# Loading the first layer's eight parameter rows from ScalarE's queue instead of the sync engine's

## The chip, the cores and the metric

The kernel runs on one core of a Trainium2 chip. The core has five engines with an instruction stream each: TensorE (PE in the rows, with its weight loads as PEld), VectorE (DVE), ScalarE (ACT), GpSimd (POOL) and the sync engine (SP). Two of these streams, SP's and ScalarE's, issue the transfers between the chip's memory and the on-chip buffers in this kernel; 16 DMA engines carry them. The metric is the device time in microseconds, the median of several runs.

## The reference

Two transformer-like blocks are applied to one sequence of 256 tokens with 2048 channels, all in float32. The first block has two layers, the second has one. What matters here is how the first one begins:

```python
def first_block(x, w_in, conv_w, conv_b, conv_ln_g, conv_ln_b, pool_w, pool_scale, g_mix,
              w_out, g_pre_mix, g_post_mix, g_pre_ffn, g_post_ffn, w_gate, w_up, w_down):
    ...
    for l in range(DEPTH):
        h = rmsnorm(x, g_pre_mix[l])
        proj = h @ w_in[l]
        y_a = conformer_conv(proj[..., :a_end], conv_w[l], conv_b[l], conv_ln_g[l], conv_ln_b[l])
        y_b = dilated_attention(proj[..., a_end:b_end], cos, sin)
        y_c = pool_mixer(proj[..., b_end:], pool_w[l], pool_scale[l])
        y = jnp.concatenate([rms_normalize(y_a), rms_normalize(y_b), rms_normalize(y_c)], axis=-1)
        y = (y * g_mix[l].astype(jnp.float32)).astype(x.dtype)
        x = x + rmsnorm(y @ w_out[l], g_post_mix[l])
        h = rmsnorm(x, g_pre_ffn[l])
        f = (jax.nn.silu(h @ w_gate[l]) * (h @ w_up[l])) @ w_down[l]
        x = x + rmsnorm(f, g_post_ffn[l])
    return x
```

The eight parameters that the change is about are `g_pre_mix`, `g_pre_ffn` (2048 numbers each), `g_mix` (2048), `conv_b`, `conv_ln_g`, `conv_ln_b`, `pool_scale` (512 each) and `conv_w` (31 taps by 512 channels) of layer 0. Of these only `g_pre_mix` is wanted at once: it scales the channels of x before the first product with `w_in`.

## The kernel before

All weights stream through a ring of four slots `WS` of 512 KB (128 partitions x 1024 numbers). Each such unit is split into a high and a low part: ScalarE copies it to `WH` in the rounded format (line 859) and VectorE forms the rest, `WL` (line 1480). TensorE then makes three products for each tile of weights and activations (line 2057). The activations `XT` are x turned by TensorE (line 2157), scaled by the column `g_pre_mix` and split in the same way: ScalarE writes the high part (line 874), VectorE the low one (line 1496).

The order of the work on each engine is written out by hand; each engine runs its own stream in that order and waits on semaphores.

At the beginning the streams are these.

- SP issues, in this order: the first constants (`C`, with the identity that TensorE needs for turning), columns 0 to 511 of x (two transfers, one for each half of the tokens), weight unit 0, then, after a wait for VectorE's clearing of `ROWS` (`s_eps`), the eight parameter rows of layer 0, then columns 512 to 1023 of x, weight unit 1, columns 1024 to 2047 of x, and units 2, 3 and so on as slots come free.
- GpSimd only passes on the arrival of x: one semaphore step when the first 512 columns are there, and all the other steps when all the rest of x is (line 1742).
- ScalarE loads its table for the square root (line 959), splits unit 0, copies the turned parameter rows to `PR` (lines 906 and 907) and then makes the high parts of the first four tiles of `XT`; then it splits unit 1, makes four more tiles, and splits three more units.
- TensorE turns the first eight 128x128 pieces of x, turns the two halves of `ROWS` (line 2177), multiplies unit 0 (24 matmuls of 256 columns), turns eight more pieces of x, multiplies unit 1, turns eight, and so on.
- VectorE clears `ROWS` and writes the small constants, makes `WL` of unit 0, and then the low parts of `XT`.

A row of parameters is first a row of `ROWS` (128 numbers in one partition) and becomes a column only by TensorE's turning. TensorE waits for all eight transfers together before it turns `ROWS`:

```python
            def layer_params(l, bank):

                pe.wait_ge(s_rows, 16 * 8 * (l + 1))
                for r in range(2):
                    pe.transpose(PS[:, bank, r * P:(r + 1) * P], ROWS[:, r, :], ident).then_inc(s_prt, 1)
```

Of the kernel before, what the change touches and what calls it, by code (L numbers as in the profile page):

```python
# [14 lines left out]
P = 128  # L15
# [75 lines left out]
TAPS = 31  # L91
# [41 lines left out]
def build(nc, a, out, stop=None):  # L133
    with ExitStack() as ctx:  # L134
        def sb(name, shape, dt=F32):
            return ctx.enter_context(nc.sbuf_tensor(name, shape, dt))

        def sem(name):
            return ctx.enter_context(nc.semaphore(name))
# [17 lines left out]
        ROWS = sb("ROWS", [P, 2, P])  # L157
# [141 lines left out]
        s_const, s_const2, s_xload, s_eps = sem("s_const"), sem("s_const2"), [sem("s_xload0"), sem("s_xload1")], sem("s_eps")  # L299
        s_rows, s_prt, s_par = sem("s_rows"), sem("s_prt"), sem("s_par")  # L300
# [37 lines left out]
        def turn_planes(queue, planes):  # L338

            for w in range(2):  # L340
                for t in range(NT):
                    queue.dma_start_transpose(plane_chan[:, w, :, t * P:(t + 1) * P], planes[:, w, t, :]).then_inc(s_turned, 16)

        @block.sync
        def _(sp):
            def load(q, i, src, width, turn=None):

                sp.wait_ge(s_lo, 4 * q + i + 1)
                if turn:
                    sp.wait_ge(s_words, turn[0])  # L350
                dst = WS[:, i % RING, :]
                if width:
                    dst = dst.rearrange("p (k n) -> p k n", n=width)
                sp.dma_start(dst, src).then_inc(s_stage[i % RING], 16)
                if turn:
                    turn_planes(sp, turn[1])

            def chunk512(q, w, c, first=False, turn=None):

                for i in range(8):  # L360
                    load(q, i, w[2 * i * P:(2 * i + 2) * P, c].rearrange("(k p) n -> p k n", p=P), CHUNK,
                         turn if turn and i == turn[2] else None)
                    if first and i == 0:
                        sp.wait_ge(s_eps, 1)
                        layer_rows(0)
                        x_columns(1, 512, 1024)
                    if first and i == 1:
                        x_columns(1, 1024, 2048)

            def out_proj(q, w):  # L370
                for c in range(2):
                    for i, kt in enumerate(OUT_ORDER):
                        load(q, 16 * c + i, w[kt * P:(kt + 1) * P, c * 1024:(c + 1) * 1024], 0)

            def down_proj(q, w, turns, between=None):

                rows = w.rearrange("(r k p) n -> r k p n", k=4, p=P)

                def four(c, r, turn=None):
                    for i in range(4):  # L380
                        load(q + r + 11 * c, i, rows[r, i, :, c * 1024:(c + 1) * 1024], 0, turn if turn and i == turn[2] else None)

                for c in range(2):
                    if c and between:
                        between()
                    for r in range(0 if c else 3):
                        four(c, r, turns.get(r))
                    with sp.Fori(0 if c else 3, FKT // 4) as r:
                        four(c, r)
# [27 lines left out]
                sp.dma_start(a_log, a["gdn_a_log_2"].to_broadcast((P, 4))).then_inc(s_rows2, 16)  # L417
                sp.dma_start(dt_bias, a["gdn_dt_bias_2"].to_broadcast((P, 4))).then_inc(s_rows2, 16)

            def layer_rows(l):  # L420

                small = [("g_pre_mix", 16), ("g_pre_ffn", 16), ("g_mix", 16), ("conv_b", 4), ("conv_ln_g", 4),
                         ("conv_ln_b", 4), ("pool_scale", 4)]
                at = 0
                for name, n in small:
                    sp.dma_start(ROWS[at:at + n, 0, :], a[name][l].rearrange("(n p) -> n p", p=P)).then_inc(s_rows, 16)
                    at += n
                sp.dma_start(ROWS[0:4 * TAPS, 1, :], a["conv_w"][l].rearrange("j (n p) -> (j n) p", p=P)).then_inc(s_rows, 16)

            def x_columns(part, c0, c1):  # L430
                for t in range(NT):
                    sp.dma_start(x[:, t, c0:c1], a["x"][0, t * P:(t + 1) * P, c0:c1]).then_inc(s_xload[part], 16)
# [3 lines left out]
            for l in range(DEPTH):  # L436
                q = l * (U_LAYER // 4)
                w = a["w_in"][l]
                for n, c in enumerate(IN_ORDER):
                    if (l, n) == (0, 1):  # L440
                        sp.dma_start(C[:, 2 * P:C_END], a["constants"][:, 2 * P:C_END]).then_inc(s_const2, 16)
                    chunk512(q + 2 * n, w, slice(c * CHUNK, (c + 1) * CHUNK), l + n == 0)
                q1 = q + U_IN1 // 4
                out_proj(q1, a["w_out"][l])
                q2 = q1 + U_OUT // 4
                def glu_loads(j, turn=None):
                    chunk512(q2 + 4 * j, a["w_gate"][l], bass.ds(j * CHUNK, CHUNK))
                    chunk512(q2 + 4 * j + 2, a["w_up"][l], bass.ds(j * CHUNK, CHUNK), turn=turn)

                glu_loads(0)  # L450
                with sp.Fori(1, 11) as j:
                    glu_loads(j, (22 * l + 2 * j - 1, plane_tok, 2))
                q3 = q2 + U_UP // 4
                if l < DEPTH - 1:
                    sp.wait_ge(s_prt, 2 * (l + 1))
                    layer_rows(l + 1)
                down_proj(q3, a["w_down"][l], {2: (22 * l + 21, plane_tok, 2)}, second_rows if l == DEPTH - 1 else None)

            q = DEPTH * (U_LAYER // 4)
# [394 lines left out]
        def _(act):  # L854
# [79 lines left out]
            def post_squares_last(q, m, n_units, bank):  # L934

                act.wait_ge(s_sf, 6 * m + 2)
                for t in range(NT):
                    for n in range(2):
                        if (t, n) == (1, 1):
                            product_done(q, 2 * n_units - 1)  # L940
                        else:
                            act.wait_ge(s_bank, 3 * m + 2 * t + n + 1)
                        act.activation(junk[3 - t][:, n * CHUNK:(n + 1) * CHUNK], PS[:, bank(1, t) + n, :], ACT.Square,  # L943
                                       accum_out=ssf[:, 3 * t + 1 + n:3 * t + 2 + n]).then_inc(s_sf, 1)
                    post_root(m, t)

            def wide_phase(q, m, n_units, first=4, last=False, bank=out_bank, params=None):
# [7 lines left out]
                splits(q, n_units + (PARAMS_AT if params else 0) + 4, 2 * n_units + (0 if last else 2))  # L955
                post_squares_last(q, m, n_units, bank)

            act.wait_ge(s_eps, 2)
            act.activation(root_junk, epsc, ACT.Sqrt)
            split(0, 0)  # L960
# [2 lines left out]
            for l in range(DEPTH):  # L963
# [6 lines left out]
                for c in range(9):  # L970
# [12 lines left out]
                    if 2 <= c < 8:  # L983
                        n = c - 2
# [1316 lines left out]
```

## Time and profile before

| what | value |
|---|---|
| median of 3 runs | 3275.39 us (3275.04 to 3275.43) |
| span of the profiled execution | 3273.7 us |
| TensorE busy | 3251.2 us, 99% of the span |
| VectorE busy | 2042.7 us, 62% |
| ScalarE busy | 1631.5 us, 50% |
| DMA, mean | 191 GB/s |
| first matmul of the first product | 10.21 us after the span's start |

The profiled execution's own time is known as its span only, 3273.7 us from the first instruction's start to the last one's end; the medians are taken from runs without a profile, and the median lies 1.7 us above the span. Busy times are shares of the span, so an engine at 99% leaves 22.5 us in which it did nothing. The rows speak of the wait ahead of an instruction group as "idle before", with an arrow to what ended it.

### The profile page before, as it was taken

Reading aid. Unit: us, or ns where it says so; the run is one execution under the profiler, and the core shown is the slowest. Engines: PE = TensorE matmul, PEld = TensorE weight load, DVE = VectorE, ACT = ScalarE, POOL = GpSimd, SP = SyncE. Lnnn points to the kernel's source line nnn. Section 1 sums busy time; section 2 is a strip of 40 time slices with the busy share of each in tenths; the row PEclk is TensorE's granted clock in tenths of the full one; section 3 lists DMA queues with packets and bytes.
Section 4 is the critical chain, followed back from the end, with each engine's and each line's share of the span. In section 5 each row is a group of like instructions: output and inputs, shape, how many; then the busy total and the mean of one; then the engine's idle time right before and its main releaser. Section 6 shows DMA issues by size and latency. Waiting matters only on the chain. (4 is left out here: it accounts for less than half of the span.)

```text
span 3273.7 us, 43491 instructions
## 1 busy us (share of the span) xinstructions
PE 3251.2 (99%) x16149; PEld 2756.5 (84%) x16149; DVE 2042.7 (62%) x2449; ACT 1631.5 (50%) x2039; POOL 263.2 (8%) x180
## 2 busy tenths in 40 slices
PE   9999999999999999999999999999999999999999
PEld 8888888888888988888888888899898888888887
DVE  6876655555444787665555544477665677777544
ACT  5565544444443556554444444365554655555443
POOL 0000011111000000001111100000000122222000
PEclk9999999999999999999999999999999999999999
DMA  7545566767756554557676766645346677777654
GB/s 231 180 136 168 180 205 207 206 206 202 218 194 193 187 181 129 173 181 205 205 205 206 207 212 198 192 150 176 116 156 204 193 218 213 218 217 216 218 194 161
DMA packets 364799, 626.70 MB, mean 191 GB/s; under 512 B 117912, under 2 KB 120445, under 8 KB 364669
## 3 DMA queue, kind: packets, MB, share of 16 engines
q1 hardware_dynamic: 359693, 615.49, 61.6%
q10 hardware_dynamic: 4976, 9.44, 0.9%
q8 instruction: 87, 1.43, 0.2%
q14 instruction: 43, 0.35, 0.0%
HBM read 599.66 MB, written 2.10 MB: 184 GB/s over the span
## 5 line engine op out<-in xcount | busy, mean ns | idle before, releaser
L1480 DVE TENSOR_TENSOR WL<-WS,WH 128x1024 fp32r<-128x1024 f32 x1120 | 1426.4, 1278 | 1083.2 <-ACT WH L859 1082.3
L859 ACT ACTIVATE WH<-WS 128x1024 fp32r<-128x1024 f32 x1120 | 1184.2, 1060 | 1502.6 <-PE PS L2057 1473.5
L2057 PE MATMUL PS<-WH,XT 128*128 128x512 f32 x5952 | 1830.4, 391 | 0.5 <-ACT XT L874 0.5
L2057 PEld LDWEIGHTS PS<-WH,XT 128*128 128x128 f32 x5952 | 1116.9, 188 | 231.9 <-issue 1.1
L2057 PE MATMUL PS<-WL,XT 128*128 128x512 f32 x2976 | 1128.7, 389 | 0.0
L2057 PEld LDWEIGHTS PS<-WL,XT 128*128 128x128 f32 x2976 | 559.0, 188 | 114.0
L2057 PE MATMUL PS<-WH,HT 128*128 128x512 f32 x2112 | 567.8, 389 | 0.0
L2057 PEld LDWEIGHTS PS<-WH,HT 128*128 128x128 f32 x2112 | 396.3, 188 | 82.5 <-DVE WL L1480 0.2
L2057 PE MATMUL PS<-XT,WH 128*128 128x256 f32 x1792 | 336.5, 286 | 2.5 <-ACT XT L874 1.4
L2057 PE MATMUL PS<-WL,HT 128*128 128x512 f32 x1056 | 327.2, 389 | 0.0
L2057 PEld LDWEIGHTS PS<-XT,WH 128*128 128x128 f32 x1792 | 283.8, 192 | 4.6 <-ACT PR L907 1.4
L2057 PE MATMUL PS<-XT,WL 128*128 128x256 f32 x896 | 254.1, 284 | 0.0
L2057 PEld LDWEIGHTS PS<-WL,HT 128*128 128x128 f32 x1056 | 198.2, 188 | 41.0
L1748 POOL COPY T<-T 128x1024 uint16<-128x1024 uint16 x44 | 66.4, 1539 | 1532.1 <-DVE T L1154 1532.1
L2057 PEld LDWEIGHTS PS<-XT,WL 128*128 128x128 f32 x896 | 172.6, 193 | 0.1
L1757 POOL COPY SCR<-SCR 128x1024 uint16<-128x1024 uint16 x44 | 44.6, 1045 | 761.6 <-ACT SCR L808 761.6
L1596 DVE SCALAR_TENSOR_TENSOR SCR<-SCR,PR 128x256 f32<-128x256 f32 x240 | 101.1, 478 | 0.0
L2057 PE MATMUL PS<-SCR 128*128 128x256 f32 (+3 forms) x648 | 100.1, 300 | 0.5 <-DVE SCR L1335 0.5
L1752 POOL COPY T<-XL 128x1024 uint16<-128x1024 uint16 x44 | 76.3, 1781 | 240.2 <-DMA XL<-T 240.2
L1763 POOL COPY T<-XL 128x1024 uint16<-128x1024 uint16 x44 | 75.6, 1764 | 247.3 <-DMA XL<-SCR 247.3
L2057 PEld LDWEIGHTS PS<-SCR 128*128 128x128 f32 (+1 forms) x648 | 88.6, 191 | 7.7 <-DVE SCR L1335 0.9
L1428 DVE SCALAR_TENSOR_TENSOR T<-T,C 128x256 f32<-128x256 f32 x176 | 73.4, 478 | 9.2 <-ACT T L815 9.2
(277 smaller groups left out, 1176.7 us busy)
## 6 DMA issues: line engine op xcount, KB each, us to landing
WS<-in_w_in_dram SPq DMA_DIRECT2D x232, 512.0 KB, 3.6
WS<-in_w_gate_dram SPq DMA_DIRECT2D x176, 512.0 KB, 3.5
WS<-in_w_up_dram SPq DMA_DIRECT2D x176, 512.0 KB, 3.7
WS<-in_w_down_dram SPq DMA_DIRECT2D x176, 512.0 KB, 4.4
WS<-in_ffn_up_dram SPq DMA_DIRECT2D x176, 512.0 KB, 4.2
WS<-in_w_out_dram SPq DMA_DIRECT2D x96, 512.0 KB, 4.1
WS<-in_ffn_down_dram SPq DMA_DIRECT2D x88, 512.0 KB, 3.7
T<-in_g_post_mix_dram ACTq DMA_DIRECT2D x4, 512.0 KB, 5.8
```

What stands on the lines that cost most here:

```text
L859: act.activation(WH[:, i % RING, :], WS[:, i % RING, :], ACT.Copy).then_inc(s_hi, 1)
L1428: ins = dve.scalar_tensor_tensor(out=f3((T2, T3)[g])[:, n, :], in0=ffn_pad[:, n, k:k + S], scalar=conv_j[:, k, g, n:n + 1], in1=f3((T2, T3 ...
L1480: dve.tensor_tensor(WL[:, i % RING, :], WS[:, i % RING, :], WH[:, i % RING, :].bitcast(F32), ALU.subtract).then_inc(s_lo, 1)
L1596: dve.scalar_tensor_tensor(out=acc[:, n, :], in0=hpad[:, n, j:j + S], scalar=w, in1=acc[:, n, :], op0=ALU.mult, op1=ALU.add).then_inc(s_cv, 1)
L1748: ins = pool.tensor_copy(plane_tok[:, w, :, :], h_words[:, :, :, w])
L1752: ins = pool.tensor_copy(hT_words[:, :, :, w], plane_chan[:, w, :, :])
L1757: ins = pool.tensor_copy(ffn_planes[:, w, :, :], ffn_words[:, :, :, w])
L1763: ins = pool.tensor_copy(pad_words[:, :, :, w], plane_chan[:, w, :, :])
L2057: return pe.matmul(o, w, r, start=start, stop=stop, skip_group_check=True)
```

## The change

SP no longer issues the eight row transfers of layer 0, nor waits for `s_eps`. ScalarE does: its stream begins with a wait for the first step of `s_eps` (VectorE's clearing of `ROWS`), then the eight transfers, and only then the table load and all that was there before. The function is moved out so that both engines can call it; the rows of layer 1 are still loaded by SP. The semaphore that counts the arrivals is the same.

```diff
+        def layer_rows(queue, l):
+
+            small = [("g_pre_mix", 16), ("g_pre_ffn", 16), ("g_mix", 16), ("conv_b", 4), ("conv_ln_g", 4),
+                     ("conv_ln_b", 4), ("pool_scale", 4)]
+            at = 0
+            for name, n in small:
+                queue.dma_start(ROWS[at:at + n, 0, :], a[name][l].rearrange("(n p) -> n p", p=P)).then_inc(s_rows, 16)
+                at += n
+            queue.dma_start(ROWS[0:4 * TAPS, 1, :], a["conv_w"][l].rearrange("j (n p) -> (j n) p", p=P)).then_inc(s_rows, 16)
+
...
                     if first and i == 0:
-                        sp.wait_ge(s_eps, 1)
-                        layer_rows(0)
                         x_columns(1, 512, 1024)
                     if first and i == 1:
                         x_columns(1, 1024, 2048)
...
-            def layer_rows(l):
...
                     sp.wait_ge(s_prt, 2 * (l + 1))
-                    layer_rows(l + 1)
+                    layer_rows(sp, l + 1)
...
+            act.wait_ge(s_eps, 1)
+            layer_rows(act, 0)
             act.wait_ge(s_eps, 2)
             act.activation(root_junk, epsc, ACT.Sqrt)
             split(0, 0)
```

SP's stream from its first transfer, before. `WS` is the ring of weight slots, `x` the input, `C` the constants, `ROWS` the parameter rows:

```order
L434 DMA C<-in_constants_dram 128x256
L432 DMA x<-in_x_dram 128x512 x2
L354 DMA WS<-in_w_in_dram 128x2x512
L426 DMA ROWS<-in_g_pre_mix_dram 16x128
L426 DMA ROWS<-in_g_pre_ffn_dram 16x128
L426 DMA ROWS<-in_g_mix_dram 16x128
L426 DMA ROWS<-in_conv_b_dram 4x128
L426 DMA ROWS<-in_conv_ln_g_dram 4x128
L426 DMA ROWS<-in_conv_ln_b_dram 4x128
L426 DMA ROWS<-in_pool_scale_dram 4x128
L428 DMA ROWS<-in_conv_w_dram 124x128
L432 DMA x<-in_x_dram 128x512 x2
```

And SP's stream from the same place, now:

```order
L432 DMA C<-in_constants_dram 128x256
L430 DMA x<-in_x_dram 128x512 x2
L364 DMA WS<-in_w_in_dram 128x2x512
L430 DMA x<-in_x_dram 128x512 x2
L364 DMA WS<-in_w_in_dram 128x2x512
L430 DMA x<-in_x_dram 128x1024 x2
L364 DMA WS<-in_w_in_dram 128x2x512 x6
```

Weight unit 1 and the later columns of x stand directly behind unit 0 now.

ScalarE's stream at its beginning, now. Before, it began with the table load of line 959:

```order
L350 DMA ROWS<-in_g_pre_mix_dram 16x128
L350 DMA ROWS<-in_g_pre_ffn_dram 16x128
L350 DMA ROWS<-in_g_mix_dram 16x128
L350 DMA ROWS<-in_conv_b_dram 4x128
L350 DMA ROWS<-in_conv_ln_g_dram 4x128
L350 DMA ROWS<-in_conv_ln_b_dram 4x128
L350 DMA ROWS<-in_pool_scale_dram 4x128
L352 DMA ROWS<-in_conv_w_dram 124x128
L959 ACT_TABLE_LOAD
L959 ACTIVATE SM<-SM 128x1
L857 ACTIVATE WH<-WS 128x1024
```

The eight transfers stand ahead of the table load and so ahead of the split of unit 0 (now line 857). The streams of TensorE and VectorE have the same instructions in the same order as before.

## Rows read from the trace of the kernel before

**Rows 1.** The page: TensorE's busy time in the whole span
```profile
PE 3251.2 (99%) x16149; PEld 2756.5 (84%) x16149; DVE 2042.7 (62%) x2449; ACT 1631.5 (50%) x2039; POOL 263.2 (8%) x180
```

**Rows 2.** TensorE's waits, whole span: us in total, times, longest us
```profile
PE PS L2157 <- POOLq L1742: 6.4, 2, 5.9
PE PS L2157 <- DVE x L1562: 3.9, 5, 0.8
PE PS L2057 <- ACT XT L874: 1.9, 6, 1.1
PE PS L2177 <- DMA ROWS<-in_conv_w_dram: 0.6, 1, 0.6
```

**Rows 3.** Timeline of TensorE: start us, us, group, idle before
```profile
5.89 1.94 PE L2157 MATMUL PS<-C,x 128*128 128x128 f32 x8 [5.89 <-POOLq L1742]
8.44 0.69 PE L2177 MATMUL PS<-C,ROWS 128*128 128x128 f32 x2 [0.61 <-DMA ROWS<-in_conv_w_dram]
10.21 0.55 PE L2057 MATMUL PS<-XT,WH 128*128 128x256 f32 x1 [1.08 <-ACT XT L874]
...
15.57 1.09 PE L2157 MATMUL PS<-C,x 128*128 128x128 f32 x8 [0.51 <-POOLq L1742]
16.42 0.36 PE L2057 MATMUL PS<-XT,WH 128*128 128x256 f32 x1
```

**Rows 4.** Timeline of ScalarE, its own queue's transfers included
```profile
0.75 1.28 ACT L959 ACT_TABLE_LOAD   x1 [0.75 <-PEq L2292]
2.04 0.20 ACT L959 ACTIVATE SM<-SM 128x1 f32<-128x1 f32 x1
7.05 1.06 ACT L859 ACTIVATE WH<-WS 128x1024 fp32r<-128x1024 f32 x1 [4.81 <-DMA WS<-in_w_in_dram]
9.17 0.22 ACT L906 ACTIVATE PR<-PS 128x64 f32<-128x64 f32 x1 [1.06 <-PE PS L2177]
9.59 1.57 ACT L874 ACTIVATE XT<-PS,PR 128x256 fp32r<-128x256 f32 x4
12.74 1.06 ACT L859 ACTIVATE WH<-WS 128x1024 fp32r<-128x1024 f32 x1 [1.58 <-DMA WS<-in_w_in_dram]
...
32.42 0.44 ACTq L968 DMA_DIRECT2D SCR<-in_pool_w_dram  x1
```

**Rows 5.** Timeline of the sync engine's issues
```profile
1.21 0.89 SPq L432 DMA_DIRECT2D x<-in_x_dram  x2
2.14 0.43 SPq L354 DMA_DIRECT2D WS<-in_w_in_dram  x1
2.62 0.46 SPq L426 DMA_DIRECT2D ROWS<-in_g_pre_mix_dram  x1
...
5.42 0.29 SPq L428 DMA_DIRECT2D ROWS<-in_conv_w_dram  x1
5.76 0.83 SPq L432 DMA_DIRECT2D x<-in_x_dram  x2
6.64 0.43 SPq L354 DMA_DIRECT2D WS<-in_w_in_dram  x1
7.11 0.94 SPq L432 DMA_DIRECT2D x<-in_x_dram  x2
```

**Rows 6.** Timeline of VectorE
```profile
0.87 0.27 DVE L1638 MEMSET ROWS<- 128x256 f32 x1 [0.87 <-PEq L2292]
...
8.14 1.23 DVE L1480 TENSOR_TENSOR WL<-WS,WH 128x1024 fp32r<-128x1024 f32 x1 [7.00 <-ACT WH L859]
...
13.83 1.23 DVE L1480 TENSOR_TENSOR WL<-WS,WH 128x1024 fp32r<-128x1024 f32 x1 [1.76 <-ACT WH L859]
```

**Rows 7.** Windows: stretch, us, busy us (count) by engine, PEclk, DMA share, GB/s
```profile
6.00:7.00 1.00, 1.00 (x6) 1.00 (x7) 0.00 (x0) 0.00 (x0) 0.00 (x0) 1.00 0.34 101
7.00:10.00 3.00, 1.52 (x6) 0.71 (x4) 1.23 (x1) 1.86 (x5) 0.00 (x0) 1.00 0.84 274
10.20:13.80 3.60, 3.59 (x16) 3.57 (x17) 1.73 (x4) 2.02 (x4) 0.00 (x0) 1.00 0.98 351
20.00:30.00 10.00, 10.00 (x85) 9.86 (x84) 8.31 (x14) 9.16 (x17) 0.00 (x0) 1.00 0.72 241
```

More of the change, by code:

```diff
@@ L418, in second_rows @@
                 sp.dma_start(dt_bias, a["gdn_dt_bias_2"].to_broadcast((P, 4))).then_inc(s_rows2, 16)
-            def layer_rows(l):
[L422 to L428, printed above, removed]
             def x_columns(part, c0, c1):
```

## The prediction, made before the changed kernel ran

> **What bounds the kernel now.** I read the page's busy times first, then the list of TensorE's waits, then the timelines of the first 17 us engine by engine, and last the windows with the DMA share. The page says that TensorE is busy for 3251.2 of 3273.7 us [rows 1]; so it does nothing for 22.5 us, and whatever a change at the beginning brings comes from these. The list of waits tells where they are. Ahead of line 2157, the turning of x, TensorE waits 6.4 us for the arrival of x in two waits, the longest 5.9, and 0.6 us for the parameter rows, once [rows 2]. The waits of 3.9 us for line 1562 stand at later layers and are not touched.
>
> TensorE's timeline shows the start as a chain. The turning of x begins at 5.89 and ends at 7.83. Then TensorE waits 0.61 us for the last parameter row (`conv_w`), turns `ROWS` from 8.44 to 9.13, waits 1.08 us for the first tile of `XT`, and starts the first product at 10.21 [rows 3]. The gap ahead of 15.57 is the second: 0.51 us for the rest of x, so unit 0 was done at 15.06. From 15.57 on TensorE runs through: 10.00 us busy of 10 between 20 and 30 us [rows 7]. Whatever brings these two points forward moves all that comes after by as much, since the stream of TensorE is unchanged and is the bound.
>
> **What is removed.** SP spends 3.14 us between the end of unit 0's issue and the start of the next x (2.62 to 5.76) [rows 5]. With this gone, the issue of x's columns 512 to 1023 moves from 5.76 to about 2.62, unit 1 from 6.64 to 3.50, the last two x transfers from 7.11 to 3.97. The issue is not the arrival, though: what these transfers win is what the DMA engines had free. Between 6 and 7 us they were busy for 0.34, between 7 and 10 us for 0.84, and from 10.2 on for 0.98 of the time [rows 7]. Free were 0.66 and 3 x 0.16 = 0.48, together 1.14 us. So the rest of x can land at most some 1.1 us earlier, not 3.1. TensorE waited for it at 15.57, and would find it at about 14.4.
>
> **What is added to ScalarE.** Its first transfer waits for VectorE's clearing of `ROWS`, over at 1.14 [rows 6]. Eight issues follow. SP's eight took 5.71 - 2.62 = 3.09 us from the first to the end of the last [rows 5]; the nearest issue of ScalarE's own queue, for `pool_w`, took 0.44 us [rows 4], and eight of these are 3.52. So they end between 4.23 and 4.66. The table load (1.28) and the small activation (0.20) come behind them, from 0.75 to 2.24 before [rows 4], and now end at 5.7 to 6.15. Queued behind is the split of unit 0, which waited 4.81 us for its data, until 7.05. That wait hides the whole of it, with 0.9 us left; without it the move would cost up to 3.9 us. I take nothing for it.
>
> **Arrival of the rows.** Before, the last row was issued at 5.42 and used at 8.44, 3.0 us later [rows 3, 5]. Now it is issued at about 4.0 and is there at 7.0 to 7.5, ahead of the end of the turning of x at 7.83. The wait of 0.61 goes. What is late next is on ScalarE: the split of unit 0 (7.05 to 8.11) and the turned rows, which TensorE would have at 7.83 + 0.69 = 8.5. ScalarE's copies and the first tile of `XT` follow, and the first product starts at 10.21 - 0.61 = 9.60. VectorE has `WL` of unit 0 at 9.37 [rows 6] and does not hold it up.
>
> **What the rows do to the loads beside them.** They travelled behind unit 0, in a stretch where the DMA engines had time; now they travel beside x and unit 0. All eight are 188 rows of 512 bytes, 94 KB. In the second from 6 to 7 us mostly they moved, 101 KB in 0.34 us of all 16 engines [rows 7]. If that work is spread evenly, everything beside it comes 0.34 us later at most. If it lies on a few engines, those carry it in up to 1.0 us, and a transfer that is spread over all 16 is over only when the slowest is: bounds 0 and 1.0 us for unit 0's arrival. Unit 0 has 9.60 - 9.37 = 0.23 us of slack on VectorE's side and 8.5 - 8.11 = 0.4 on ScalarE's. I take 0.4 us of delay, near the even spread since most of x and of unit 0 is under way before the last and largest row is issued: VectorE's `WL` comes at 9.77, and the first product at about 9.8. The start is won by 0.4 us; by the bounds it is between 0.6 won and 0.2 lost (9.37 + 1.0 = 10.37, against 10.21).
>
> The share of 0.34 in that stretch, about 5 engines of 16, is what few engines busy with many small rows would give [rows 7]. The Trainium skill, DMA: Bandwidth & Descriptors, "Why a DMA increments its semaphore by 16 and not by 1", says that a transfer runs on the largest number of engines up to 16 that divides its slowest dimension: 4 for the 124 partitions of `conv_w`, 16 for a weight unit. The same page, "Queues, rings and completion order", has each DMA engine take turns between the two queues packet by packet, so the moved rows do slow what SP has issued. By these two rules the delay of unit 0 goes to the 1.0 us and the start is at 10.37; that speaks against the change and is the third case below.
>
> **The pace of the first matmuls.** Between 10.2 and 13.8 TensorE made 16 matmuls in 3.60 us, 0.225 each, and between 20 and 30 us 85 in 10, 0.118 each, while the granted clock is listed as 1.00 in both [rows 7]. If the quicker pace sets in at the same moment as before, the 0.4 us won are used at the slow pace: some 2 matmuls, worth 2 x 0.118 = 0.24 us. If it moves along, they are worth 0.4. I take 0.3.
>
> **The sum.** Start 0.3, plus the gap before 15.57: unit 0 is done at 15.06 - 0.3 = 14.76, the rest of x is there at 14.4 to 14.8, so the 0.51 us go as well. Together 0.8 us. Unit 1's `WL` was ready at 15.06 [rows 6] and is wanted at 16.42 - 0.8 = 15.6; it comes earlier too, since ScalarE waited 1.58 us for unit 1's data, until 12.74 [rows 4]. On its own time the profiled execution goes from a span of 3273.7 to 3272.9. The median of runs lies 1.7 us above the span and I let that distance stand: 3275.39 - 0.8 = 3274.6 us.
>
> **The rivals.** All times are for the median.
>
> - *The forecast*, 0.3 to 1.2 us less: 3274.6, between 3274.2 and 3275.1. Chance 0.55.
> - *More comes back.* The rows cost the other loads nothing, the start comes 0.8 us earlier (10.21 to the 9.37 at which `WL` is there, if the turning ends sooner as well), the quick pace moves with it, and 0.51 is added: 1.3 us, up to 1.8 if the half pace gets shorter by 4 matmuls x 0.107 = 0.4. 3273.6 to 3274.1. For it: the 3 us of SP's time that are free. Against it: the DMA share of 0.98 from 10.2 on. Chance 0.15.
> - *Hidden anyway.* Unit 0 is delayed until the start stands at 10.2 to 10.4, or the rest of x comes no earlier than 15.5, since the same bytes pass the same engines. One of the gains is lost and the other halved: -0.2 to 0.3 us less, 3275.1 to 3275.6. By this the change does what it says, and nothing follows. For it: the low share between 6 and 7 us, when few engines seem to carry the rows [rows 7]. Chance 0.2.
> - *Slower.* ScalarE is the place. If its issues take 0.6 us each instead of 0.44, they end at 5.9 and table load and activation at 7.4; the split of unit 0 starts later than 7.05 from an issue of 0.55 us on. With unit 0 late by 1.0 in addition (8.05), the two do not add, since ScalarE waits for the later one. The start then is at 10.4 to 10.8, the gap at 15.57 closes for as much, and the rest, up to 0.6, stays: 3275.6 to 3276.2. For it: these would be the first issues of that queue in the run, of which there is no row. Against it: the 0.44 us later in the same queue [rows 4]. Chance 0.1.
>
> **Numbers.** From 3273.6 to 3275.7 lie the forecast, nearly all of the second case and the third; the median of before itself moves by 0.4 us from run to run. I give 3273.4 to 3276.0. What a measurement of this kernel can tell from no change is about 0.2%, 6.5 us, and every case lies inside that. Up to the second turning TensorE idles 5.89 + 0.61 + 1.08 + 0.51 = 8.1 us [rows 3], and of the 5.89 nothing goes while x is issued where it was, so a gain over 6.5 is nearly shut out; and no step here puts 6.5 us in its way. Faster 0.01, within 0.98, slower 0.01.
>
> **What would show it.** In the profile of the changed kernel: ScalarE's eight issues from 1.15 to about 4.5, with the table load behind them; the split of unit 0 at 7.1 to 7.5 with a wait for its data ahead of it (if there is none, the slower case is at work); the turning of `ROWS` directly behind that of x, at about 7.9, with no wait; the first product at 9.8; no wait for line 1742 ahead of the second turning of x, which begins at 14.7. Wrong it would be if unit 0 landed at 8 or later, if the second turning still waited, or if the time moved by more than 1.8 us in either direction, which would have to come from somewhere past 17 us.

## The result and the profile after

| kernel | median | lowest to highest | runs |
|---|---|---|---|
| before | 3275.31 us | 3274.95 to 3277.04 | 21 |
| changed | 3281.19 us | 3280.06 to 3282.38 | 21 |

The changed kernel is 5.9 us slower; the ratio is 1.0018, with a 95% interval of 1.0012 to 1.0024. The time lies far outside the range that was given (3273.4 to 3276.0), on the other side of the forecast. The profiled execution has a span of 3278.8 us, 5.1 us more than before; with 3280.57 us it was one of the quicker of the 21, 0.6 us under their median.

TensorE's waits over the whole span of the changed kernel, in us in total, times and the longest:

```profile
PE PS L2177 <- DMA ROWS<-in_conv_w_dram: 6.4, 1, 6.4
PE PS L2157 <- POOLq L1742: 5.9, 1, 5.9
PE PS L2157 <- DVE x L1562: 3.9, 5, 0.8
PE PS L2057 <- ACT XT L872: 1.8, 5, 1.1
```

Against [rows 2], the second wait for x is gone, as forecast (6.4 us in two waits have become 5.9 in one), and the wait for `conv_w` has grown from 0.6 to 6.4 us. The wait for line 1562 is as it was. TensorE's timeline of the start shows the same:

```profile
5.90 1.94 PE L2157 MATMUL PS<-C,x 128*128 128x128 f32 x8 [5.90 <-POOLq L1742]
14.24 0.69 PE L2177 MATMUL PS<-C,ROWS 128*128 128x128 f32 x2 [6.40 <-DMA ROWS<-in_conv_w_dram]
16.01 0.55 PE L2057 MATMUL PS<-XT,WH 128*128 128x256 f32 x1 [1.08 <-ACT XT L872]
...
21.00 0.28 PE L2057 MATMUL PS<-XT,WH 128*128 128x256 f32 x1
21.12 1.03 PE L2157 MATMUL PS<-C,x 128*128 128x128 f32 x8
21.91 0.36 PE L2057 MATMUL PS<-XT,WH 128*128 128x256 f32 x1
```

The turning of x begins where it did (5.89 in [rows 3]); the turning of `ROWS` is at 14.24 instead of 8.44, and the first product at 16.01 instead of 10.21: 5.80 us later. The second turning follows unit 0 without a gap. Unit 1 starts at 21.91 instead of 16.42, so 5.5 us of the 5.8 are left there, and 5.1 at the end.

ScalarE's timeline, its own transfers included, and below it SP's:

```profile
1.18 0.41 ACTq L350 DMA_DIRECT2D ROWS<-in_g_pre_mix_dram  x1
...
3.79 0.32 ACTq L350 DMA_DIRECT2D ROWS<-in_pool_scale_dram  x1
4.13 0.45 ACTq L352 DMA_DIRECT2D ROWS<-in_conv_w_dram  x1
4.61 1.28 ACT L959 ACT_TABLE_LOAD   x1 [4.61 <-issue]
5.90 0.20 ACT L959 ACTIVATE SM<-SM 128x1 f32<-128x1 f32 x1
8.02 1.06 ACT L857 ACTIVATE WH<-WS 128x1024 fp32r<-128x1024 f32 x1 [1.91 <-DMA WS<-in_w_in_dram]
14.96 0.22 ACT L904 ACTIVATE PR<-PS 128x64 f32<-128x64 f32 x1 [5.89 <-PE PS L2177]
```

```profile
2.61 0.94 SPq L430 DMA_DIRECT2D x<-in_x_dram  x2
3.60 0.43 SPq L364 DMA_DIRECT2D WS<-in_w_in_dram  x1
4.08 1.26 SPq L430 DMA_DIRECT2D x<-in_x_dram  x2
5.38 21.90 SPq L364 DMA_DIRECT2D WS<-in_w_in_dram  x6
```

ScalarE's issues end at 4.58 and the table load and activation at 6.1, as forecast, and the split of unit 0 still waits for its data, 1.91 us, so ScalarE is not the cause. Unit 0 is there at 8.02 instead of 7.05 [rows 4]; in the runs below that leave the same loads behind it, it is there by 7.2 in one and at 8.1 in another. `conv_w` is issued at 4.13, 1.3 us earlier than before [rows 5], and its last row is awaited until 14.24: 10.1 us from issue to use, against 3.0.

The windows (stretch, us, busy us and count of TensorE, its weight loads, VectorE, ScalarE and GpSimd, the granted clock, the DMA share, GB/s), in the stretches of [rows 7]:

```profile
6.00:7.00 1.00, 1.00 (x6) 1.00 (x7) 0.00 (x0) 0.11 (x1) 0.00 (x0) 1.00 1.02 376
7.00:10.00 3.00, 0.84 (x4) 0.43 (x3) 0.89 (x1) 1.06 (x1) 0.00 (x0) 1.00 1.05 378
```

The free share of the DMA engines, 0.66 and 0.16 before, is used up, as forecast: the large loads fill it. What the forecast did not ask is where the rows pass in it. The packets by queue say it. q1 is SP's queue and q10 ScalarE's; the columns are packets, MB, and the packets' time as a share of 16 engines. First from 2 to 8.2 us, then from 8.2 to 13.7:

```profile
q1 hardware_dynamic: 996, 1.76, 84.6%
q10 hardware_dynamic: 130, 0.03, 2.7%
```

```profile
q1 hardware_dynamic: 796, 2.02, 99.8%
q10 hardware_dynamic: 125, 0.06, 3.9%
```

The 64 rows of the seven short transfers (0.03 MB) pass until 8.2. The 124 rows of `conv_w` (0.06 MB) need from 8.2 to 13.7, 5.5 us, while SP's queue takes 99.8% of the engines. The rows' own share is 3.9% of 16 engines, 0.2 us of the 5.5 if all 16 carried them and 0.9 us if four did: they do not take long, they wait.

### The profile page after: what moved, and what is told of

The parts are those of the page before. It is cut to its first block and busy times, and to the rows that moved or that the text cites. A ratio compares the mean times of both kernels' runs of the same rounds, so it can differ in the third digit from the quotient of the medians.

```text
span 3278.8 us, 43491 instructions
## 1 busy us (share of the span) xinstructions
PE 3251.3 (99%) x16149; PEld 2757.2 (84%) x16149; DVE 2042.8 (62%) x2449; ACT 1631.0 (50%) x2039; POOL 262.0 (8%) x180
```

## The experiments

Each run is named by its medians beside the kernel before on the same chip. Theory T came out of the rows above: `conv_w`'s 124 rows lie on few DMA engines, and each row waits there for a turn beside SP's large packets. Theory Q was the rival: ScalarE's queue as a whole gets little beside SP's.

The Trainium skill, DMA: Bandwidth & Descriptors, "Queues, rings and completion order", says that each DMA engine takes turns between the queues, and "Why a DMA increments its semaphore by 16 and not by 1" that the number of engines is the largest up to 16 that divides the slowest dimension. By it 124 rows lie on 4 engines, 31 each; the runs below with 62, 64 and 128 rows agree in their order.

The traces can be asked for the number of engines as well. In the first 30 us ScalarE's queue has 128 packets where it carries the seven short transfers alone (the run with `conv_w` on SP's queue). With `conv_w` added it has 256 in the changed kernel, 256 with 62 and 62 rows, 283 with 64 and 60, and 272 with 128. So `conv_w` has 128, 128, 155 and 144 packets, which is its rows and 4, 4, 31 and 16 more. That is one more packet for each engine of each transfer, if the engines are 4, 2 + 2, 16 + 15 and 16; the seven short ones fit too, with 64 rows and 64 more (3 x 16 + 4 x 4).

**`conv_w` in 64 and 60 rows.**

```diff
-            queue.dma_start(ROWS[0:4 * TAPS, 1, :], a["conv_w"][l].rearrange(...)).then_inc(s_rows, 16)
+            taps = a["conv_w"][l].rearrange("j (n p) -> (j n) p", p=P)
+            for r0, r1 in ((0, 64), (64, 4 * TAPS)):
+                queue.dma_start(ROWS[r0:r1, 1, :], taps[r0:r1]).then_inc(s_rows, 16)
```

> The changed kernel with conv_w of both layers loaded in two transfers, of 64 and 60 rows, instead of one of 124. Theory T (turn-taking on few engines: each DMA engine takes one small row of ScalarE's queue per large packet of SP's queue, about 0.23 us a turn, and the 124 rows of conv_w lie on 4 engines, 31 each; 64 and 60 rows lie on 16 and 15 engines, 4 each): conv_w takes 8 turns instead of 31, the wait of 6.4 us ahead of the turning of ROWS falls below 1.5 us, the first product starts at 10.0 to 10.8 us and the median is 3274.6 to 3275.6. Theory Q (ScalarE's queue as a whole gets a small share beside SP's, 0.058 us a row whatever its shape): the wait stays at 6 us or grows, first product at 16, 3281.

Measured: 3277.53 us beside 3275.24, ratio 1.0008 (0.9998 to 1.0017). The profiled execution had the turning of `ROWS` at 12.67 and the first product at 14.44, and was the slowest of ten (3280.55). It holds something else besides: a fall of the clock that the profiled executions of the kernels before and after do not show there, in the stretch from 2141 to 2145 us (columns as above):

```profile
2141.00:2145.00 4.00, 3.89 (x19) 3.76 (x20) 3.78 (x8) 2.02 (x4) 0.00 (x0) 0.61 0.02 4
```

That fall cost this execution some 1.6 us (4 us at 0.61). Packets by queue from 8.3 to 12.2 us:

```profile
q1 hardware_dynamic: 531, 1.46, 97.2%
q10 hardware_dynamic: 163, 0.07, 6.0%
```

Theory Q falls: by the medians 3.6 us of the 5.9 have gone, by the shape of one transfer, and the rows of `conv_w` pass in 3.9 us instead of 5.5. In the profiled execution only 1.6 us of the 5.8 had gone at the first product; what was better in the others no trace shows. Theory T's size was off as well: it had left out that `conv_w`'s rows do not begin before 8.2, and 8 turns were to take far less than 3.9 us.

**`conv_w` in 62 and 62 rows.** The same edit with the cut at 62.

> The changed kernel with conv_w in two transfers of 62 rows each. Theory T: 62 is divided by 2 and by no other number up to 16, so each transfer lies on 2 engines, and the two on the same ones: 62 turns instead of 31, until SP's loads run out at about 18 us. conv_w lands at 18 to 20 us instead of 14, the first product starts at 20 to 22, the median is 3285 to 3288. Theory Q: the same bytes and rows, no change: first product at 16, 3281. The same number of transfers as with 64 and 60 rows, so the extra issue (0.4 us) tells nothing.

Measured: 3284.04 us beside 3275.24, ratio 1.0027 (1.0015 to 1.0038), 2.9 us slower than the changed kernel. TensorE's timeline:

```profile
6.57 1.94 PE L2159 MATMUL PS<-C,x 128*128 128x128 f32 x8 [6.57 <-POOLq L1744]
17.51 0.69 PE L2179 MATMUL PS<-C,ROWS 128*128 128x128 f32 x2 [9.00 <-DMA ROWS<-in_conv_w_dram]
19.28 0.55 PE L2059 MATMUL PS<-XT,WH 128*128 128x256 f32 x1 [1.08 <-ACT XT L874]
```

The same bytes in the same number of transfers as with 64 and 60, and the turning is 4.8 us later. Packets by queue from 8.6 to 17 us:

```profile
q1 hardware_dynamic: 1239, 2.87, 91.1%
q10 hardware_dynamic: 132, 0.06, 2.6%
```

The rows of `conv_w` now take 8.4 us. Theory T is borne out in direction and nearly in size (17.5 where 18 to 20 was expected, 3284.04 where 3285 to 3288 was).

**`conv_w` in one transfer of 128 rows.**

```diff
+            if l == 0:
+                taps = a["conv_w"].rearrange("l j (n p) -> (l j n) p", p=P)
+                queue.dma_start(ROWS[:, 1, :], taps[0:P]).then_inc(s_rows, 16)
...
```

> The changed kernel with conv_w of layer 0 loaded as one transfer of 128 rows (four rows of layer 1's taps behind it, which nothing reads) instead of 124, so that it divides by 16. Theory T (few engines): 8 turns on each of 16 engines instead of 31 on 4: from about 8.4, where conv_w's rows begin in all runs so far, they last 1.5 to 2.5 us, the turning of ROWS starts at 10.5 to 11.5 instead of 14.24, the first product at 12.3 to 13.3, median 3277.3 to 3278.3. Theory D (rows wait for their descriptors to be generated among those of the large transfers, at about 0.03 us a row as in the run with 64 and 60 rows): 128 rows last 3.7 us, turning at 12.7, product at 14.5, median 3279.5. Theory Q (neither): as with 124 rows, 3281.2.

Measured: 3277.72 us beside 3275.39, ratio 1.0007 (0.9998 to 1.0017). The turning of `ROWS` is at 10.71, the first product at 12.48. The packets from 8.1 to 10.4 us and the wait:

```profile
q1 hardware_dynamic: 350, 0.80, 94.0%
q10 hardware_dynamic: 155, 0.07, 10.3%
```

```profile
10.71 0.69 PE L2181 MATMUL PS<-C,ROWS 128*128 128x128 f32 x2 [2.87 <-DMA ROWS<-in_conv_w_dram]
12.48 0.55 PE L2061 MATMUL PS<-XT,WH 128*128 128x256 f32 x1 [1.08 <-ACT XT L876]
```

Four rows more, and they pass in 2.3 us instead of 5.5, with a share of 10.3% of the engines instead of 3.9%. Theory T holds here, in its numbers too, and theory D (3.7 us, turning at 12.7) does not. One thing stays open between the two: 64 and 60 rows also mean 8 turns, and took 3.9 us. So the shape of `conv_w` (124 rows) is 3.5 us of the loss; the rest, 2.3 us, is that the rows begin at about 8.1 and still need 2.3 us.

**`conv_w` back on SP's queue, the seven others on ScalarE's.**

```diff
                     if first and i == 0:
+                        sp.wait_ge(s_eps, 1)
+                        conv_rows(sp, 0)
```

> The changed kernel with conv_w of layer 0 alone back on SP's queue at its old place behind weight unit 0; the other seven rows stay on ScalarE's queue. Theory T: the seven take 7 turns at most on any engine and are in by 8 us, conv_w goes in the order of SP's own queue ahead of the next x and is in by 8: first product at 9.8 to 10.4, median 3274.4 to 3275.4. Theory Q: the seven rows still wait for their share, 64 of 188 rows: first product at 11 to 12, median 3276 to 3277.

Measured: 3275.22 us beside 3275.24, ratio 1.0001 (0.9991 to 1.0010). In the profiled execution x was there at 6.76 instead of 5.89, the turning of `ROWS` at 8.86 (0.15 us of wait, for `pool_scale`), the first product at 10.63, a little later than expected, and the wait for the rest of x was gone. The loss is bound to `conv_w`; moving the seven others costs and brings nothing that can be measured.

**`conv_w` alone on ScalarE's queue, first of all.** The counterpart: the seven others stay on SP.

> The kernel before with conv_w of layer 0 alone moved to ScalarE's queue, where it is issued first, at 1.2; the seven others stay on SP's queue behind unit 0, and SP's later loads move up by one issue only. In the run with conv_w first its rows passed between 2.4 and 4, since SP had little under way yet: here they do the same, and the seven (64 rows) pass behind unit 0 at 6 to 7. Turning of ROWS at 7.9 to 8.4, first product at 9.6 to 10.2, median 3274.6 to 3275.3. If conv_w on ScalarE's queue is slow in whatever place, turning at 12 or later and 3278 or more.

Measured: 3275.07 us beside 3275.56, ratio 0.9998 (0.9989 to 1.0008); turning at 8.62, first product at 10.38. Its rows, with 128 packets, passed between 2 and 4.4 us:

```profile
q1 hardware_dynamic: 373, 0.57, 68.0%
q10 hardware_dynamic: 128, 0.06, 11.0%
```

So `conv_w` on that queue is not slow as such. Its 124 rows pass in at most 2.4 us while SP's queue takes 68% of the engines, against 5.5 us at 99.8%. The seven others were in later than expected (turning at 7.9 to 8.4).

**`conv_w` first of the eight.**

```diff
+            queue.dma_start(ROWS[0:4 * TAPS, 1, :], a["conv_w"][l].rearrange(...)).then_inc(s_rows, 16)
             at = 0
             for name, n in small:
...
-            queue.dma_start(ROWS[0:4 * TAPS, 1, :], a["conv_w"][l].rearrange(...)).then_inc(s_rows, 16)
```

> The changed kernel with conv_w issued first of the eight on ScalarE's queue. The same rows and the same number of turns (38 on the busiest engines), but they begin at 2.4 instead of 8.4, beside x and unit 0, whose packets are of 2 KB and not of 4 KB, and seven short transfers follow. By turn-taking at 0.13 us a turn conv_w is through at 6.5 and the rest at 8 to 9: first product at 10.5 to 11.5, median 3275.5 to 3276.5. x and unit 0 may land up to 1 us later. If what counts is the number of transfers ahead in the queue and not conv_w's turns, all the same: the last row lands at 8 to 9. If the queue is slow as such: 3281.

Measured: 3275.70 us beside 3275.39, ratio 1.0001 (0.9992 to 1.0011). The turning is at 9.72, after 1.9 us of wait for the last of the eight (`pool_scale`), and the first product at 11.49, as expected. `conv_w` itself was quicker than expected: 124 packets of the queue had passed by 4, where its end was put at 6.5. A change of order alone takes back 5.6 of 5.9 us by the medians, and 4.5 of 5.8 at the first product of the profiled execution.

**SP's later loads held back until the rows are in.**

```diff
                     if first and i == 0:
+                        sp.wait_ge(s_rows, 16 * 8)
                         x_columns(1, 512, 1024)
```

> The changed kernel with SP waiting, behind weight unit 0, until all eight rows have landed, before it issues the rest of x and unit 1. Both theories say that the large transfers beside the rows are what holds them up: the rows are in by 8 us and the first product starts at 9.7 to 10.3. The rest of x is issued at about 7.8 instead of 5.76 (kernel before), so it lands at 17 to 17.5 and TensorE waits some 2 us ahead of the second turning: median 3276.5 to 3277.3. A third theory, that transfers of ScalarE's queue are slow by themselves at the start of a run (queue first used, many small rows): the rows land at 14 as before and then all else is late as well: median above 3284.

Measured: 3279.44 us beside 3275.24, ratio 1.0012 (1.0002 to 1.0021). The part on the rows came out as expected: with nothing behind unit 0, `conv_w` was in by 7.86 and the first product was at 9.62. Packets from 6 to 7.4 us, ScalarE's queue before SP's this time:

```profile
q10 hardware_dynamic: 159, 0.07, 17.6%
q1 hardware_dynamic: 35, 0.05, 8.8%
```

Up to 6 us ScalarE's queue has as many packets here (97) as in the changed kernel (96). The other 159, `conv_w` among them, take 1.4 us with nothing of SP's beside them but the end of unit 0, and 7.7 us in the changed kernel. So it is SP's loads beside them that hold up the rows. Unit 0, with the same eight transfers beside it, was there when it was in the kernel before (7.05):

```profile
7.03 1.06 ACT L858 ACTIVATE WH<-WS 128x1024 fp32r<-128x1024 f32 x1 [1.05 <-DMA WS<-in_w_in_dram]
```

The time was missed by over 2 us. TensorE waited 2.48 us for the rest of x, and after that its granted clock was lower (second row, 17.1 to 20.5):

```profile
17.17 1.83 PE L2158 MATMUL PS<-C,x 128*128 128x128 f32 x8 [2.48 <-POOLq L1743]
```

```profile
14.70:17.10 2.40, 0.00 (x0) 0.00 (x0) 1.23 (x1) 0.64 (x1) 0.00 (x0) 1.00 0.98 340
17.10:20.50 3.40, 3.33 (x16) 3.33 (x17) 1.02 (x3) 1.89 (x5) 0.00 (x0) 0.54 1.05 405
```

0.54 is nearly the lower of the two levels (1.2 of 2.4 GHz) for 3.4 us; that costs about half of them, 1.6 us, and the expectation had left it out. The profiled execution, with 3278.16 us, is explained by this and the later turning; why the median lies 1.3 us above it is open.

**The first product no longer waits for `conv_w`.** All transfers as in the changed kernel; `conv_w` of layer 0 has a semaphore of its own.

```diff
-                pe.wait_ge(s_rows, 16 * 8 * (l + 1))
-                for r in range(2):
+                pe.wait_ge(s_rows, 16 * (8 * l + 7))
+                for r in range(2 if l else 1):
...
+            def conv_params():
+                pe.wait_ge(s_cw, 16)
+                pe.transpose(PS[:, 7, P:2 * P], ROWS[:, 1, :], ident).then_inc(s_prt, 1)
```

> The changed kernel, all transfers as in it, but conv_w of layer 0 counts on a semaphore of its own: TensorE turns the first half of ROWS as soon as the seven other rows are in, and the half with conv_w only behind the second turning of x. If the whole loss is TensorE's wait for conv_w, the turning of ROWS starts at 8.3 to 9.3 (the seven others have landed by then in the runs so far), the first product at 10 to 10.8, and the median is 3274.8 to 3275.6, though conv_w still lands at 14. If the rows beside the loads cost time in another way as well (weights later through the whole start), it stays above 3277.

Measured: 3275.64 us beside 3275.39, ratio 1.0000 (0.9991 to 1.0010).

```profile
5.64 1.94 PE L2164 MATMUL PS<-C,x 128*128 128x128 f32 x8 [5.64 <-POOLq L1749]
9.02 0.47 PE L2186 MATMUL PS<-C,ROWS 128*128 128x128 f32 x1 [1.44 <-DMA ROWS<-in_pool_scale_dram]
10.41 0.55 PE L2064 MATMUL PS<-XT,WH 128*128 128x256 f32 x1 [0.91 <-ACT XT L873]
```

With the same eight transfers on the same queue the loss is gone: the span is 3273.8 beside 3273.7 us, the first product 0.20 us behind that of the kernel before. So the loss is that wait, as far as a median can tell (0.25 us, with an interval of some 3 us to either side). The seven short transfers, too, are late (9.02; `pool_scale` was issued at 3.79).

**Three transfers ahead of `conv_w` instead of seven.** The four transfers of 4 rows went back to SP, and ScalarE's small activation stood ahead of `conv_w`'s issue.

> What is still open is why conv_w's rows begin only at about 8.3 in the changed kernel, though it is issued at 4.13. Here the changed kernel with the four short transfers (conv_b, conv_ln_g, conv_ln_b, pool_scale, 4 rows each) back on SP's queue behind unit 0, and with the table load and the small activation ahead of conv_w's issue on ScalarE, so that conv_w is issued at about 4.1 again but has three transfers ahead of it in its queue instead of seven. Theory R (each transfer of ScalarE's queue waits for about one large transfer of SP's): conv_w's rows begin at 6.0 to 6.6, last some 5 us by their 31 turns, so the turning of ROWS starts at 11.5 to 12.5 and the first product at 13.3 to 14.3; median 3278.3 to 3279.5. Theory L (a lag of 4 us between issue and rows on this queue, whatever is ahead): rows begin at 8, turning at 14 to 14.5, product at 16, median 3281.

Measured: 3275.44 us beside 3275.56, ratio 1.0000 (0.9990 to 1.0009); turning at 8.84, first product at 10.60. The experiment did not do what it was to do: ScalarE issued `conv_w` while its table was loading,

```profile
2.56 1.28 ACT L963 ACT_TABLE_LOAD   x1 [2.56 <-issue]
2.63 0.51 ACTq L354 DMA_DIRECT2D ROWS<-in_conv_w_dram  x1
```

so the issue was at 2.63 and not at 4.1, and the rows passed by 7.7. Packets from 6 to 7.7 us:

```profile
q1 hardware_dynamic: 302, 0.51, 87.7%
q10 hardware_dynamic: 130, 0.06, 12.6%
```

The rows began at about 6, within theory R's range and within a lag of some 4 us from their issue, so the two aren't told apart by it; but they then passed in at most 1.7 us, where theory R had 5. That speaks against a fixed price for a turn: 31 rows on each engine took 1.7 us with SP's queue at 87.7% and 5.5 at 99.8%, and what sets the price isn't shown.

It tells something of the late beginning too. In both kernels 94 to 96 packets of ScalarE's queue have passed at 6 us, which is the number of the three transfers of 16 rows (48 rows and 48 more). In the changed kernel the four of 4 rows (32 packets) come next, until about 8.1, and `conv_w` behind them; here `conv_w` comes next, and at once. By these counts some 2 us of the late beginning are the four short transfers ahead of it. Why nothing behind the first three passes before 6 stays open.

**A candidate to beat both.** `g_pre_mix` alone is issued from ScalarE's queue and turned by itself; the seven others go on SP's queue behind the last columns of x and are turned later.

```diff
-            layer_rows(act, 0)
+            first_row(act)
...
                         x_columns(1, 1024, 2048)
+                        layer_rows(sp, 0)
...
+                    pe.wait_ge(s_gr, 16)
+                    pe.transpose(PS[:, 7, 0:16], ROWS[0:16, 0, :], ident[0:16, 0:16]).then_inc(s_prt, 1)
```

> A candidate to beat both kernels. Only g_pre_mix, which the first product needs, is issued from ScalarE's queue at the beginning and is turned by itself (16 rows); the seven others go on SP's queue behind the last columns of x, and are turned behind the third turning of x. TensorE has g_pre_mix by 5 us, so it waits for x, unit 0 and ScalarE alone: first product at 9.5 to 10.0, no wait ahead of the second turning; the turning of all rows (0.4 us) lies later in the stream instead of ahead of the product. Median 3274.0 to 3274.8, that is 0.5 to 1.2 us under the kernel before. If x and unit 0 land later by what is issued earlier behind them, as in the run with conv_w on SP (x at 6.76), nothing is won: 3275.0 to 3275.4.

Measured: 3275.23 us beside 3275.39, ratio 0.9999 (0.9990 to 1.0009), scattered from 3273.88 to 3276.51; the first product at 9.73, as expected, unit 1 at 15.66 instead of 16.42, the span 3272.6. The median is not the 3274.0 to 3274.8 that was expected. The second turning did not wait:

```profile
14.87 1.04 PE L2169 MATMUL PS<-C,x 128*128 128x128 f32 x8
```

> The candidate again, timed in more rounds: g_pre_mix alone on ScalarE's queue and turned by itself, the seven others on SP's queue behind the last columns of x. Its profile had the first product at 9.73 and a span 1.1 us under the profiled run of the kernel before, but ten runs scattered from 3273.9 to 3276.5. If the start is worth 1.1 us in most executions, the median lies 0.4 to 1.2 us under that of the kernel before on the same chip; if something of later in the program takes it back (a short fall of the clock, as between 2100 and 2200 us in the profiled run with 64 and 60 rows), the difference is within 0.4 us.

Measured again: 3274.88 us beside 3275.56, ratio 0.9998 (0.9989 to 1.0007), first product at 9.83; the 0.7 us lie within the 0.4 to 1.2 expected.

> The same with g_pre_mix on SP's queue, between the first columns of x and unit 0. One issue (0.45 us) ahead of unit 0, so unit 0 lands at 7.3 to 7.7 and the first product starts at 9.7 to 10.1; nothing is on ScalarE's queue at the beginning. Median within 0.4 us of the candidate with g_pre_mix on ScalarE's queue. If the queue itself matters even for one short transfer, the difference is larger.

Measured, with `g_pre_mix` on SP's queue: 3275.39 us beside 3275.56, ratio 0.9999 (0.9990 to 1.0008). Unit 0 was there at 8.06 and the first product at 10.43, later than expected, and the median lies 0.5 us from the candidate's, a little more than the 0.4 expected. None of the three is told apart from the kernel before by its interval. The start is better by 0.4 to 0.5 us in the profiles with ScalarE's queue, and no faster version is claimed.

## Why the prediction was wrong

The median was to be 3274.6 and is 3281.19. By the prediction's own steps:

- *What bounds the kernel, and the chain at the start*: right. What came at the start moved the end by nearly as much (5.8 us at the first product, 5.1 at the end of the profiled execution). The distance between time and span stood: in the 21 executions of the changed kernel it is 1.8 to 1.9 us.
- *What is removed*: right. The later loads moved up as said (2.61, 3.60, 4.08 for 2.62, 3.50, 3.97), and filled what the DMA engines had free. The 0.51 us ahead of the second turning went, but in this kernel they would have gone in any case, since unit 0 was not done before 21.28. That the later x really comes earlier is shown by the runs in which the first product was not late: the second turning began without a wait at 14.87 with `g_pre_mix` alone on ScalarE's queue, where 14.7 was forecast.
- *What is added to ScalarE*: right in its numbers (issues until 4.58, table load and activation until 6.1, for 4.23 to 4.66 and 5.7 to 6.15) and hidden as said. The slower case, which was built on this place, did not happen.
- *Arrival of the rows*: this is the step that failed. "Now it is issued at about 4.0 and is there at 7.0 to 7.5" carried the 3.0 us between issue and use over from SP's queue [rows 3, 5]. There the rows stood in the same queue as the large loads, behind unit 0 and ahead of all later ones, and `conv_w` was in by 8.44 though the next x was issued directly behind it, at 5.76. On ScalarE's queue they lost that place: the later x and unit 1 stood beside them, and not behind. `conv_w` was awaited until 14.24. The run with SP's loads held back shows it from one side (7.86), the run with `conv_w` back on SP's queue from the other (8.86), and the run in which the product doesn't wait for `conv_w` leaves no loss that can be measured (3275.64).
- *What the rows do to the loads beside them*: unit 0 came 0.97 us later, near the upper bound of 1.0 and not at the 0.4 taken. The rows are not shown to be the reason. With the same rows on ScalarE's queue and SP's later loads held back unit 0 was there at 7.03, and with no rows on that queue but the later loads moved up (`g_pre_mix` on SP's queue) at 8.06, of which 0.5 is its own later issue. The loads issued behind unit 0 are at least a part of it, and the sum had no term for them. It cost nothing here, for the rows came later still. The question was also put one way round only. The share of 0.34 between 6 and 7 us was read rightly, as few engines with many small rows [rows 7], and used only for what the rows do to unit 0. The same fact, turned round, is the greater part of the loss: few engines mean many turns for the rows. With 62 and 31 turns by the Trainium skill's rule `conv_w` passed in 8.4 and 5.5 us, and with 8 turns in 3.9 (two transfers) and 2.3 (one). The order is that of the turns, the price of a turn isn't constant.
- *The pace of the first matmuls*: the quicker pace moved by more than the start. It set in about 3.8 us after the first product before (near 14.0) and about 4.7 us after it now (near 20.7), with the granted clock listed as 1.00 all the while, so unit 0 took 5.27 us (16.01 to 21.28) for 4.85 before. These 0.42 us went against the change, where the forecast had taken 0.1 us off its gain.
- *The rivals*: none named the wait for the rows themselves. "Slower" looked at ScalarE's time, "hidden anyway" at unit 0 and x. All four took it that the rows arrive. The bound for a wait on a queue not seen in the trace should have gone as far as the loads beside it last: the DMA engines were known to be busy for 0.98 of the time from 10.2 to 13.8 at the least [rows 7], and that far the upper end of the arrival should have gone. A turning at 13.8 instead of 8.44 is 5.4 us more, a median of 3280.8, close to the 3281.19 measured.
- *The signs of being wrong*: two came, unit 0 at 8.02 (the bound was 8) and a median moved by more than 1.8 us. The second was to come "from somewhere past 17 us" and came from before 17, so this sentence was wrong with the step on the arrival.
- *The chances*: 0.98 for a change within 0.2% was right (0.18%), though just so. "No step here puts 6.5 us in its way" was nearly wrong for the reason above.

What is shown and what isn't: that the loss is the wait for `conv_w`, that it depends on SP's loads beside it, and that it depends on how the rows divide, is shown by runs. That the dependence on the number of rows comes from 2, 4 and 16 engines is the reading that fits the four durations in their order and the packet counts exactly; no row here lists engines one by one. What a turn costs is open (31 rows on each engine in 1.7 to 5.5 us, 8 in 2.3 and 3.9), and so is why nothing behind the three transfers of 16 rows passes before 6 us.

## What to carry to other kernels

In this kernel a transfer that moved to another queue lost its place ahead of what was issued later on the old one. If the old queue has large loads, ask how long the moved one may wait beside them, and take as the upper bound the time until those loads run out. Small rows whose number divides badly (62, 124) were hit hardest; 128 rows, or an earlier issue, or a consumer that doesn't wait for all of them, each took back most of the loss here (3.5, 5.6 and 5.6 us of 5.9, by the medians).

## What the runs showed of the hardware that was not expected

- Between 2 and 4.4 us, with SP's queue at 68% of the engines, `conv_w`'s 124 rows passed in at most 2.4 us; between 8.2 and 13.7, with it at 99.8%, in 5.5.
- A transfer of n rows on ScalarE's queue has more packets than rows: 4 more for 124 rows, 16 for 128, 31 for 64 and 60, 4 for 62 and 62. That is one for each engine that would carry it, by the reading above.
- ScalarE issued a transfer that stood behind a table load while the table was still loading (2.63, in a load from 2.56 to 3.84).
- After 2.48 us without a matmul, TensorE's granted clock was 0.54 from 17.1 to 20.5 us. In the profiled execution with 64 and 60 rows it also fell, to 0.61, from 2141 to 2145 us, which costs some 1.6 us. With `g_pre_mix` on SP's queue it was 0.87 from 2130 to 2140; the other profiled executions have 1.00 there. Whether such falls are why executions of one kernel differ by 1 or 2 us isn't shown.
